# Two blocks of a language model on one core: two buffers per stage, rounded operands and split level sums in the first layer's recurrence

## The reference, cut to what matters

```
def hgrn2_chunkwise(q, logf, k, v):
    ...
    bcum = jnp.cumsum(lc, axis=3)
    pair = jnp.exp(jnp.minimum(bcum[..., :, None, :] - bcum[..., None, :, :], 0.0))
    att = jnp.einsum('bhnik,bhnjk,bhnijk->bhnij', qc, kc, pair)
    ...
    d, inc = inp
    return d[..., None] * state + inc, state
    ...
yb = rmsnorm(ob, gn) * jax.nn.silu(bg)
```

## Time and profile before

| what | value |
|---|---|
| median of 3 runs | 3088.03 us (3085.52 to 3089.1) |
| the profiled execution's own time | 3087.3 us |
| its span, first to last instruction | 3085.6 us |
| the recurrence, from 352 us to 474 us | 122 us |
| PE busy in it | 84.94 us |
| DVE busy in it | 93.92 us |
| ACT busy in it | 60.27 us |
| POOL busy in it | 45.31 us |
| the last 1341 us (expert rows) | DMA engines 0.97 busy |

### The profile page before, as it was taken

One profiled execution on the slowest core, in us unless ns is written; L12 is line 12 of the kernel. 1 busy time (PEld: TensorE's weight loads), 2 busy tenths in 40 slices (PEclk: granted clock), 3 DMA queues, 4 the chain that ended last, 5 costly groups with the idle time before them and its releaser, 6 DMA issues.

```text
span 3085.6 us, 30864 instructions
## 1 busy us (share of the span) xinstructions
PE 2526.9 (82%) x12334; PEld 1796.6 (58%) x12334; DVE 1600.6 (52%) x2125; ACT 951.2 (31%) x1580; POOL 692.3 (22%) x751
## 2 busy tenths in 40 slices
PE   7999878899998989999889047777777587777776
PEld 6997757799898889898679012222222232222222
DVE  4656485444455444356543866666544544444443
ACT  4467354444775444345443000000100001000001
POOL 5012230000000000430000043334333243333331
PEclk9999999999999989899999579999999899999999
DMA  5643204455444534243444099999999999999997
GB/s 189 210 151 129 91 1 165 150 178 184 158 141 153 184 111 164 84 137 110 133 141 136 14 414 422 422 421 421 422 421 421 404 398 421 422 421 422 421 421 298
DMA packets 200270, 779.52 MB, mean 253 GB/s; under 512 B 16548, under 2 KB 20864, under 8 KB 134080
## 3 DMA queue, kind: packets, MB, share of 16 engines
q0 software_dynamic: 74400, 537.15, 42.0%
q1 hardware_dynamic: 125728, 240.40, 23.5%
HBM read 775.40 MB, written 2.10 MB: 252 GB/s over the span
## 4 chain that ended last, share of the span: by engine, by line
PE 56%; DMA 34%; DVE 6%; ACT 2%; issue 2%; POOL 0%; DVEq 0%; ACTq 0%; SPq 0%
PE bank L1541 55%; DMA VROW<-in_peer_v_dram,WORK 31%; DMA UROW<-in_peer_u_dram,WORK 2%; DVE HL L997 1%; DVE WORK L1306 0%; DVE BIG L1319 0%; PE bank L1636 0%; DVE WORK L1431 0%; DVE WORK L1434 0%; DVE BIG L1432 0%; DVE WL L966 0%; DVE HL L1010 0%; DVE WORK L1433 0%; DVE WORK L1430 0%; POOL UROW L469 0%
## 5 line engine op out<-in xcount | busy, mean ns | idle before, releaser
L1541 PE MATMUL bank<-VROW,WORK 128*128 128x512 f32 x2048 | 939.3, 603 | 430.1 <-DMA VROW<-in_peer_v_dram,WORK 406.8
L1541 PEld LDWEIGHTS bank<-VROW,WORK 128*128 128x128 f32 x2048 | 371.8, 191 | 997.0 <-issue 855.1
L1509 DVE CUSTOM_DVE_ANT_0 BIG<-UROW,bank 128x2048 f32<-128x2048 f32 x256 | 585.5, 2288 | 602.3 <-DMA UROW<-in_peer_u_dram,WORK 601.3
L966 DVE TENSOR_TENSOR WL<-RAW,WH 128x1024 fp32r<-128x1024 f32 (+2 forms) x464 | 544.9, 1182 | 585.5 <-ACT WH L535 584.7
L535 ACT ACTIVATE WH<-RAW 128x1024 fp32r<-128x1024 f32 (+2 forms) x464 | 467.4, 1023 | 519.0 <-PE bank L1541 518.4
L1541 PE MATMUL bank<-HH,WH 128*128 128x256 f32 x2112 | 605.4, 287 | 11.5 <-DVE WL L966 11.5
L1541 PE MATMUL bank<-HL,WH 128*128 128x256 f32 x2112 | 601.5, 285 | 0.0
L1541 PE MATMUL bank<-HH,WL 128*128 128x256 f32 x2112 | 601.3, 285 | 0.0
L1541 PEld LDWEIGHTS bank<-HH,WH 128*128 128x128 f32 x2112 | 408.7, 194 | 16.1 <-issue 15.5
L1541 PEld LDWEIGHTS bank<-HL,WH 128*128 128x128 f32 x2112 | 409.0, 194 | 0.0
L1541 PEld LDWEIGHTS bank<-HH,WL 128*128 128x128 f32 x2112 | 408.9, 194 | 0.0
(11 more groups left out here) (299 smaller groups left out, 1694.8 us busy)
## 6 DMA issues: line engine op xcount, KB each, us to landing
RAW<-in_w_in_odd_dram SPq DMA_DIRECT2D x64, 1024.0 KB, 5.1
RAW<-in_w_in_even_dram SPq DMA_DIRECT2D x48, 1024.0 KB, 5.0
RAW<-in_w_in_dram SPq DMA_DIRECT2D x44, 1024.0 KB, 4.9
RAW<-in_w_out_even_dram SPq DMA_DIRECT2D x16, 1024.0 KB, 5.0
RAW<-in_w_out_odd_dram SPq DMA_DIRECT2D x16, 1024.0 KB, 5.0
RAW<-in_w_out_dram SPq DMA_DIRECT2D x16, 1024.0 KB, 5.2
RAW<-in_peer_wq_dram SPq DMA_DIRECT2D x16, 1024.0 KB, 5.1
UROW<-in_peer_u_dram,WORK POOLq DMA_INDIRECT x256, 27.0
```

Source lines behind the costliest of these rows:

```text
L966: dve.tensor_tensor(WL[:, sl:sl + 2, 0:w], raw[:, k0:k0 + 2, 0:w], WH[:, sl:sl + 2, 0:w].bitcast(F32), ALU.subtract).then_inc(s["wl_done"], 1)
L1509: dve.tensor_tensor_reduce(out=JUNK[:, n % 2, :], in0=UROW[:, b, :], in1=TT, op0=ALU.mult, op1=ALU.add, scale=1.0, scalar=0.0, accum_out=D ...
L1541: return pe.matmul(dst, lhsT, rhs, start=start, stop=stop, skip_group_check=True)
```

## The change

It has three parts, all in the recurrence of the first layer.

1. *Rounded operands for the level sums.* The 0/1 masks are copied once by ACT, in the middle of the input projection (four copies, 128x1280 in all), into `MSR`, which holds them as `F32R`. `LFT` is rounded by ACT's copy, and a new DVE instruction per stage (`decays_low`, 128x128) takes what rounding left into `LFL`. `level_sums` is now four one-pass products of 128x512 (rounded part and rest, for each bank).
2. *Level sums split.* DVE masks bank 2 into `B_AM[u % 2]` and bank 3 into `AMB`, and adds the two (128x512, both from SBUF). The reduce is gone. PE's `values` multiplies by the four remaining 128x128 parts and accumulates them. `products` waits for the masks alone, `values` for the add.
3. *Two buffers* for `qe` (`B_QE`) and `am` (`B_AM`), and new loops. PE does `level_sums` one stage ahead and `values` one behind; DVE does `qe` one stage ahead; the head's normalisation moves from even to odd iterations, behind the add. POOL's `B_KE` has seven parts, not eight.

```diff
@@ rounded views over parts of BIG and WORK
+            LFL1 = rounded_sb("LFL1", P)
+            MSR = rounded_sb("MSR", 1280)
+            LFT2 = rounded_sb("LFT2", 2 * P)
+            LFL0 = rounded_sb("LFL0", P)
...
-        B_KE = [WORK[:, 2048:3072], BIG[:, 4, :]]
+        B_KE = [WORK[:, 2048:2944], BIG[:, 4, 0:896]]
+        LFL = [LFL0[:, :], LFL1[:, :]]
+        B_QE = [WORK[:, 1024:2048], BIG[:, 2, :]]
+        B_AM = [WORK[:, 3072:3584], WORK[:, 3584:4096]]
@@ POOL
-                kk = k.unsqueeze(1).broadcast_to([P, 8, P])
-                pool.tensor_tensor(ke, ex, kk, ALU.mult).then_inc(s["b_ke"], 1)
+                kk = k.unsqueeze(1).broadcast_to([P, LEVELS, P])
+                pool.tensor_tensor(ke, ex[:, 0:LEVELS, :], kk, ALU.mult).then_inc(s["b_ke"], 1)
@@ ACT
+                if place == A_PREPARE:
+                    act.wait_ge(s["masks"], 2)
+                    act.activation(MSR[:, 1024:1152], MS[:, 6, :], ACT.Copy).then_inc(s["b_ms"], 1)
...
+                    act.activation(MSR[:, 0:896], MS.rearrange("p l i -> p (l i)"), ACT.Copy).then_inc(s["b_ms"], 1)
...
+            log_decays(1)
+            decays(0)
+            y_high_eight(0, 0, BIG[:, 3:5, :])
+            for i in range(2 * B_HEADS + 4):
+                head = (i - 3) // 2
+                if i >= 3 and i % 2 == 1 and head < B_HEADS:
+                    head_square(head)
+                if i + 2 < 2 * B_HEADS:
+                    log_decays(i + 2)
                 if i + 1 < 2 * B_HEADS:
-                    log_decays(i + 1)
...
+                    decays(i + 1)
+                if i % 2 == 1 and i < 2 * B_HEADS:
+                    cross(i // 2)
+                if i >= 3 and i % 2 == 1 and head < B_HEADS:
+                    head_rms(head)
+                if i >= 4 and i % 2 == 0:
+                    y_high(8 + (i - 4) // 2)
@@ DVE
+            def decays_low(u):
+                dve.wait_ge(s["b_lf"], u + 1)
+                dve.tensor_tensor(LFL[u % 2], bank[4][:, (u % 2) * P:(u % 2 + 1) * P], LFT[:, u % 2, :].bitcast(F32),
+                                  ALU.subtract).then_inc(s["b_ll"], 1)
...
+            def masked(u):
...
+                am = B_AM[u % 2]
+                dve.tensor_tensor(am, bank[2], MK[:, 0:4, :].rearrange("p l i -> p (l i)"), ALU.mult)
+                dve.tensor_tensor(AMB[:, :], bank[3], MK[:, 4:8, :].rearrange("p l i -> p (l i)"), ALU.mult)\
+                    .then_inc(s["b_msk"], 1)
+                dve.wait_ge(s["b_msk"], u + 1)
+                dve.tensor_tensor(am, am, AMB[:, :], ALU.add).then_inc(s["b_am"], 1)
...
-                    dve.tensor_reduce(B_SUM[:, i % 2, :], am.rearrange("p (l i) -> p i l", l=8), AX.X, ALU.add)\
-                        .then_inc(s["b_sum"], 1)
...
+            for i in range(2 * B_HEADS + 4):
+                if i + 2 < 2 * B_HEADS:
+                    decays_low(i + 2)
+                if i + 1 < 2 * B_HEADS:
+                    query(i + 1)
+                if i < 2 * B_HEADS:
+                    masked(i)
+                if i >= 3 and i % 2 == 1 and (i - 3) // 2 < B_HEADS:
+                    normed((i - 3) // 2)
+                if i >= 4 and i % 2 == 0:
+                    y_low(8 + (i - 4) // 2)
@@ PE
-                mm(bank[0][:, :], LFT[:, m, :], msf[:, 0:512], True, True)
-                mm(bank[1][:, 0:384], LFT[:, m, :], msf[:, 512:896], True, True)
-                mm(bank[1][:, 384:512], LFT[:, m, :], (GT if m == 0 else LE)[:, :], True, True)\
-                    .then_inc(s["b_es"], 1)
...
+                mm(bank[0], LFT[:, m, :], MSR[:, 0:512], True, False)
+                mm(bank[0], LFL[m], MSR[:, 0:512], False, True)
...
+                mm(dst, LFT[:, m, :], ends, True, False)
+                mm(dst, LFL[m], ends, False, True).then_inc(s["b_es"], 1)
...
-                mm(o[:, ts], v, B_SUM[:, m, :], True, m == 0).then_inc(s["b_lev"], 1)
+                for j in range(4):
+                    ins = mm(o[:, ts], v, B_AM[m][:, j * P:(j + 1) * P], j == 0, m == 0 and j == 3)
+                ins.then_inc(s["b_lev"], 1)
...
+            log_decays(1)
+            level_sums(0)
+            for i in range(2 * B_HEADS + 2):
+                if i + 2 < 2 * B_HEADS:
+                    log_decays(i + 2)
+                if i + 1 < 2 * B_HEADS:
+                    level_sums(i + 1)
+                if i < 2 * B_HEADS:
+                    products(i)
+                if i >= 3 and i % 2 == 1:
+                    square_sums((i - 3) // 2)
                 if 0 <= i - 1 < 2 * B_HEADS:
-                    products(i - 1)
...
+                    values(i - 1)
```

More of the change, by code:

```diff
@@ L790, in head_rms, with cross @@
                 act.activation(BRS, BRS, ACT.Exp, scale=-0.5).then_inc(s["b_rs"], 1)
-            for i in range(2 * B_HEADS + 6):
-                if i + 1 < 2 * B_HEADS:
-                    log_decays(i + 1)
[L795 to L805, removed]
-                if i >= 7 and i % 2 == 1:
-                    y_high(8 + (i - 7) // 2)
-                if i >= 4 and i % 2 == 0 and i < 2 * B_HEADS + 4:
-                    head_square((i - 4) // 2)
-                if i >= 5 and i % 2 == 1 and i < 2 * B_HEADS + 5:
-                    head_rms((i - 5) // 2)
+            def cross(h):
+                act.wait_ge(s["b_cross"], h + 1)
+                if h >= 1:
+                    act.wait_ge(s["b_ov"], h)
+                act.activation(CX, bank[6][:, 0:P], ACT.Copy).then_inc(s["b_cx"], 1)
+            log_decays(1)
[7 more added lines that the diff above has]
+                    log_decays(i + 2)
+                if i + 1 < 2 * B_HEADS:
+                    decays(i + 1)
[5 more added lines that the diff above has]
+                    y_high(8 + (i - 4) // 2)
             phase("even_out")
@@ new lines, in normed @@
+            def normed(h):
+                c = 8 + h
+                dve.wait_ge(s["b_rs"], h + 1)
+                y_wait(c)
+                y = YB[:, c % 2, :]
+                link(dve.scalar_tensor_tensor(y, bank[5 + 2 * (h % 2)][:, 0:T], COLS[:, V_GN:V_GN + 1], BRS,
+                                              ALU.mult, ALU.mult))
+                dve.tensor_tensor(y, y, chan(11, h), ALU.mult).then_inc(s["y_ready"], 1)
+            decays_low(0)
+            y_low_eight(0, 0, BIG[:, 3:5, :])
@@ new lines, in _ @@
+            decays_low(1)
+            query(0)
+            for i in range(2 * B_HEADS + 4):
[9 more added lines that the diff above has]
+                    y_low(8 + (i - 4) // 2)
@@ L1779, in values @@
                 o = bank[5 + 2 * (h % 2)]
[L1780 removed]
+                pe.wait_ge(s["b_am"], u + 1)
                 if m == 0 and h >= 2:
@@ L1814, in square_sums @@
                 mm(bank[5 + 2 * (h % 2)][:, T:2 * T], ONES[:, :], BSQ, True, True).then_inc(s["b_ss"], 1)
-            for i in range(2 * B_HEADS + 4):
+            log_decays(1)
[5 more added lines that the diff above has]
+                    level_sums(i + 1)
                 if i < 2 * B_HEADS:
-                    level_sums(i)
-                if i + 1 < 2 * B_HEADS:
-                    log_decays(i + 1)
+                    products(i)
+                if i >= 3 and i % 2 == 1:
+                    square_sums((i - 3) // 2)
                 if 0 <= i - 1 < 2 * B_HEADS:
-                    products(i - 1)
-                if 0 <= i - 2 < 2 * B_HEADS:
-                    values(i - 2)
-                if i >= 4 and i % 2 == 0:
-                    square_sums((i - 4) // 2)
+                    values(i - 1)
             phase("even_out")
```

99 lines of the change are left out of this document (47 added, 52 removed).

## The result

| | before | after |
|---|---|---|
| median | 3088.57 us (3085.52 to 3089.4, 4 runs) | 3065.77 us (3061.85 to 3066.65, 4 runs) |
| the profiled execution | 3087.3 us, span 3085.6 | 3061.85 us, span 3059.9 |
| products(5) | 390.70 us | 385.29 us |
| five heads, products(5) to products(15) | 67.94 us, 13.59 each | 52.48 us, 10.50 each |
| products(15) to `even_out` | 15.66 us | 15.06 us |

A forecast was written before the change was run, and what follows sets the result against it. No engine is busy throughout the recurrence; waits between engines, DVE-POOL exclusion and TensorE's clock set its pace. Terms -0.2 to stage 5, -5.0 in five heads, -0.6 in the tail: -5.8 on 3087.3 gives 3081.5 us, range 3072 to 3091.

The forecast's parts named there:

- Who goes first: Odd-stage `qe` against POOL's multiply: POOL first 12.0 us a head; DVE first 10.5, the next 12.1; taken 11.7.
- The clock: TensorE idle some 3 us before odd products: low clock costs 1.5 us in three heads of five, 0.9 a head.
- a mixed head: Head length with either engine first, 11.3 to 12.0 us, taken as 11.7; 12.6 with the clock's 0.9, against 13.59.
- Stages 1 to 4: Stages without normalisation on DVE: nearly all of POOL's 2.07 us added, 5.3 us a stage against 5.0 to 5.1.
- products(0): Start of the first products: rounded sums and an earlier log-decay copy bring it from 363.65 to about 361.8 us.
- the loop and its members: From odd products: cross product 2.3 us, tables until 6.0, exponentials 7.15, then `qe` and POOL's multiply start together.
- the locks of add and `y_low`: DVE instructions with two SBUF inputs and POOL's multiply exclude each other; `y_low` takes 2.33 us beside it, 0.41 otherwise.
- the tail: From products(15) to PE's start of the next phase: 15.1 us against 15.66, -0.6.
- C: Rival: POOL first against add, `y_low` and `qe` every time, heads 14.5 us, kernel slower at 3094 us; chance 0.13.
- Rounded sums: `level_sums` on PE: rounded 128x512 passes, four make 0.92 us; about 0.8 us of PE saved per stage.
- Rival A: Everything better: DVE wins each start, clock stays up, heads 10.7 us, kernel 3072 us; chance 0.15.

The follow-up runs named there:

- POOL-first trace: Changed kernel with one waited-for 128x128 clearing (memset) on DVE between the exponentials' wait and `qe` of each stage: 3085.95 us, ratio 0.9992.
- its filler: Six unused plain 128x384 PE products ahead of odd products from stage 5 on, added to the changed kernel with the waited-for DVE clearing: 3080.71 us, ratio 0.9978.
- rms later: Changed kernel with `head_rms` and what follows moved behind the next odd stage's exponentials: 3066.54 us, ratio 0.9929.
- `y_low` behind `qe`: Changed kernel with `head_rms` and what follows behind the next odd stage's exponentials, and `y_low` moved behind the query: 3063.64 us, ratio 0.9917.

## Why the prediction was wrong

- **Who goes first** failed, the step "If DVE is first: ... but add, `y_low` and `qe` of the next stage are pushed back by the same amount, and the head after it comes out at 12.1. So 11.3 to 12.0; I take 11.7." Both lengths were right in their own case, 10.5 against 10.53 measured, 12.0 against 11.8 to 12.0 at full clock. Wrong was that DVE first in one head must lose the next. The work pushed back has room, if only just: it ends 5.99 us after the odd products began, and `head_rms`, which DVE must wait for, at 6.08. From there the normalisation, `decays_low` and the query follow as in the head before, and DVE is at its query when the exponentials end, every time. The two masks take 0.60 + 0.71 us from start to start, against my 1.42; in the even stage that difference alone, 0.11 us, is as much as the room. The reduce used it up: at stage 9 it ends at 406.91, where `head_rms` had ended at 406.25. Size: 11.7 - 10.53, 1.2 us a head, 6 in all.
- **The clock** failed with it. I charged 0.9 us a head for an idle PE of 3 us; that idle time belongs to POOL first (3.24 measured, clock 0.89 in the window), and there the low clock cost 1.5 to 1.7 us a head, close to the 1.5 that I took for a slow one. With DVE first PE waits 0.95 and 0.80 us and the clock stays at 1.00. Size: 0.9 a head, 4.5 in all. I had added it to a mixed head instead of tying it to one of the two orders. The Trainium skill (TensorE: Matmul & The Clock Gate, HAM oscillation) describes short bursts with idle gaps that start at the low clock; the POOL-first trace agrees, with an idle stretch of 3.24 us ahead of products that take 3.45 us for 2.02, and so does its filler, which brings the window from 0.89 to 1.00.
- **Stages 1 to 4** failed for the same reason: I put nearly all of POOL's 2.07 us on top of DVE's work, 5.3 us a stage. DVE is first in each of them (362.88 against 362.92 in the first), they took 4.0 to 4.7, and POOL's multiply lies beside the masks; with POOL first (the first clearing) they take 4.95 from stage 1 on. Size: 3.5 us by products(4), which began at 379.22. Stage 5 with the first normalisation took 6.1 us where I had left 7.5, 1.4 more. products(5) came at 385.29 instead of 390.5.
- **products(0)** came at 361.52, 361.8 predicted, and that was luck. Of the 2.1 us gained there 1.0 arose ahead of the recurrence, which the sum did not have, and with plain level sums it comes at 360.92, so the rounded sums, one of my two reasons, did not bring it forward.
- **Right**: the loop and its members, the locks of add and `y_low`, the tail (15.1 predicted, 15.06), that C would not come. The add took 0.69 alone (0.65), `decays_low` 0.28 (0.27). Rounded sums were right as a small item: without them the loss is 2.4 us.
- Rival A had the head right (10.7) but not the first stages, and with 0.15 I held it far too low: it lay not in luck but in which of two engines is 0.04 us ahead.

The sum in its place: -5.4 to products(5), -15.5 in the heads, -0.6 in the tail, -21.5.

## What to carry to other kernels

Where two engines that lock each other out are released by one semaphore, work out both orders as two cases with their own idle time and clock, and then count how long before the release each engine is free: the one that is late loses by a whole instruction. A lighter instruction ahead of such a meeting may be worth many times its own saving. Parts of a change may hang together: the lighter sum was worth nothing on the old loops, while in the new kernel more than half of the gain goes without either it or the second buffer. And if something is put in to keep an engine busy, look whether it runs past the wait that it fills. An idle stretch of TensorE is priced together with the order that makes it, never as a term of its own.

## What the runs showed of the hardware

- 0.04 us decide: DVE at 403.07, POOL at 403.11, and POOL's multiply takes 3.14 us for its own 2.1, so it stands behind nearly all of DVE's 1.22. The Trainium skill (SBUF — State Buffer, Who interferes with whom) says that issue order and not the kind of operation decides who blocks; both orders are seen here, `qe` at 1.22 and 2.96 us, the multiply at 3.14 and 2.10 us.
- A mask with one operand in PSUM is not held up by POOL's multiply: 0.68 us beside it.
- Where PE's waits in a settled head were 0.80 and 0.95 us (after), 1.1 (rms later) or up to 1.6 (`y_low` behind `qe`), the granted clock of 380 to 440 us stayed at 1.00. With waits of 3.2 us in each head it was 0.89, single groups at the lower level (3.45 us for 2.02). Between these the length of the wait alone does not tell: with one `qe` buffer waits of 2.2 to 2.5 us stand in heads of 1.00 and of 0.87, with the reduce waits of 1.9 and 2.9 us in heads of 0.81 to 0.99.
- A clearing with a semaphore behind it cost DVE 0.2 us for 0.17 of work; one of 0.11 us that nothing waits for did not move the query behind it.
